# Expert rows weighted at the copy and added by indirect DMA into token sums in memory

## What is computed

```
g_idx = argmax(g_logits)                      # one of 4 groups per token
top_v, top_i = top_k(softmax(e_sel), 2)       # two of its 4 experts
combine = p_gsel * one_hot(g_idx) * e_w       # weight of each of the two
for grp in range(4):
    hid = silu(t @ w_gate[grp]) * (t @ w_up[grp])
    out = out + (hid * combine[..., None]) @ w_down[grp]
x = x + out
return rmsnorm(x, final_norm_g)
```

## Time and profile before

| | |
|---|---|
| median of 3 runs | 701.88 us (701.83 to 702.55) |
| the profiled execution | 701.97 us |
| its span on the core | 699.9 us |
| granted TensorE clock, mean | 0.993 of full speed |
| PE busy | 97% of the span |
| DVE, ACT, POOL busy | 40%, 21%, 11% |
| DMA traffic | 111.9 MB, 160 GB/s over the span |
| chain that ended last | PE 90%, DMA 4%, DVE 2% |

### The profile page before, as it was taken

One profiled execution on the slowest core, in us unless ns is written; L12 is line 12 of the kernel. 1 busy time (PEld: TensorE's weight loads), 2 busy tenths in 40 slices (PEclk: granted clock), 3 DMA queues, 4 the chain that ended last, 5 costly groups with the idle time before them and its releaser, 6 DMA issues.

```text
span 699.9 us, 8436 instructions
## 1 busy us (share of the span) xinstructions
PE 678.7 (97%) x3398; PEld 332.1 (47%) x3398; DVE 282.1 (40%) x669; ACT 144.3 (21%) x308; POOL 78.9 (11%) x106
## 2 busy tenths in 40 slices
PE   7999999999999999999999999999999999999993
PEld 4644445453557665444444555555564333333331
DVE  3107599935244665313120312323335821212156
ACT  3011251003053454211011122221111110101113
POOL 3000082312020000000000000000001110110063
PEclk9999999999999999999999999999999999999997
DMA  8803140301136513300009410630169999999673
GB/s 296 309 0 121 62 178 1 121 1 62 61 120 186 181 61 121 120 1 0 1 1 377 178 45 1 240 121 35 55 210 329 312 365 388 370 381 387 238 233 127
DMA packets 69939, 111.90 MB, mean 160 GB/s; under 512 B 5648, under 2 KB 43780, under 8 KB 69900
## 3 DMA queue, kind: packets, MB, share of 16 engines
q1 hardware_dynamic: 65724, 96.16, 39.7%
q0 software_dynamic: 4176, 15.21, 5.9%
HBM read 101.90 MB, written 9.46 MB: 159 GB/s over the span
## 4 chain that ended last, share of the span: by engine, by line
PE 90%; DMA 4%; DVE 2%; ACT 1%; POOL 1%; issue 1%; SPq 0%; DVEq 0%; POOLq 0%; ACTq 0%
PE bank L1931 19%; PE bank L2200 16%; PE bank L1806 11%; PE bank L2278 8%; PE bank L1835 5%; PE bank L1941 5%; PE bank L2288 2%; PE bank L1977 2%; PE bank L2308 2%; PE bank L2166 2%; DMA W<-y_dram,A 2%; PE bank L1963 2%; PE bank L1788 1%; PE bank L2144 1%; PE bank L2153 1%; PE bank L2049 1%
## 5 line engine op out<-in xcount | busy, mean ns | idle before, releaser
L2200 PE MATMUL bank<-W,n_sb 128*128 128x512 f32 x256 | 114.3, 596 | 0.0
L1931 PE MATMUL bank<-hT,W 128*128 128x512 f32 x240 | 104.5, 593 | 0.0
L1806 PE MATMUL bank<-W,A 128*32 128x512 f32 x672 | 84.8, 594 | 1.5 <-DVE A L1175 1.5
L2200 PEld LDWEIGHTS bank<-W,n_sb 128*128 128x128 f32 x256 | 47.3, 190 | 52.4 <-issue 52.3
L1931 PEld LDWEIGHTS bank<-hT,W 128*128 128x128 f32 x240 | 45.2, 190 | 56.1 <-issue 55.8
L2278 PE MATMUL bank<-hT,W 128*128 128x512 f32 x128 | 56.1, 592 | 0.0
L1441 DVE SCALAR_TENSOR_TENSOR A<-A,pc 128x511 f32<-128x511 f32 (+29 forms) x60 | 51.6, 860 | 2.0
L698 POOL TENSOR_TENSOR rstd<-ss,mhalf 128x1 f32<-128x1 f32 x14 | 7.7, 550 | 357.8 <-DVE ss L1068 199.0
L1806 PEld LDWEIGHTS bank<-W,A 128*32 128x32 f32 x672 | 23.1, 110 | 49.6 <-issue 47.6
L2278 PEld LDWEIGHTS bank<-hT,W 128*128 128x128 f32 x128 | 24.3, 190 | 28.1 <-issue 27.5
L1835 PE MATMUL bank<-Dn,A 128*32 128x512 f32 x264 | 36.3, 595 | 0.0
(11 more groups left out here) (311 smaller groups left out, 844.1 us busy)
## 6 DMA issues: line engine op xcount, KB each, us to landing
W<-in_w_gate_dram SPq DMA_DIRECT2D x14, 1024.0 KB, 5.4
W<-in_w_up_dram SPq DMA_DIRECT2D x14, 1024.0 KB, 10.1
Dn<-in_w_down_dram SPq DMA_DIRECT2D x11, 1024.0 KB, 14.6
W<-in_w_in_dram SPq DMA_DIRECT2D x5, 2048.0 KB, 8.6
W<-in_w_xkv_dram SPq DMA_DIRECT2D x4, 2048.0 KB, 7.9
hT<-in_w_down_dram SPq DMA_DIRECT2D x5, 1024.0 KB, 12.6
y_dram<-A POOLq DMA_DIRECT2D x10, 512.0 KB, 7.3
W<-in_w_out_dram SPq DMA_DIRECT2D x2, 2048.0 KB
```

What stands on the lines that cost most here:

```text
L1806: mm = nc.tensor.matmul(PS[2 + b][r, :], xgT[:, b, c, r], gu_at[GU_HOME[e]][:, c, :], start=c == 0, stop=c == DC - 1)
L1931: mm = nc.tensor.matmul(bank[0:w, 0:n], lhs, src[:, c, 0:n], start=c == 0, stop=c == DC - 1)
L2200: mm = nc.tensor.matmul(PS[(k + (2 if base else 0)) % 4][:, :], src[:, c, t * P:(t + 1) * P], W[:, (n_load + n) % SLOTS, c, :], start=firs ...
```

## The change

The expert rows are multiplied by their weight where they are copied out of PSUM (`y_half`: a scale on ACT, a multiplication on DVE). The weights of a pass's rows, `row_w`, come from 24 small products (`weigh_rows`): the 0/1 matrices that chose the rows, times each token's weights split into three float16 parts, put together again by DVE (`row_weights`).

Instead of `y_dram` there is `sum_dram`, 512 token rows and 128 spare rows. SP stores the residual tiles into it beside the normed ones, and once more as a filling of the spare rows. POOL adds each pass but the last to it by indirect DMA with an add: rows 0 to 95, then rows 96 to 127, since one token may be in both. Rows without a token go to spare rows of their own. Each add waits for the one before, and the gather of pass p+5 is issued between the two adds of pass p. The copies of pass p wait for the adds of pass p-2. At the end SP loads the four tiles back into `x_sb` plainly; the eight gathers and eight weighted adds are gone. Only the last pass is spread by PE (`LATE = 1`), with 0/1 matrices that need no turning; pass 10's second half is copied by DVE and not by ACT. DVE's chain of small steps in `combine` that worked out slots (L1236 to L1269) goes. The overflow branch is rewritten to add in the same way, and SP's part of it is unrolled.

```diff
-LATE = 2
-ZERO_ROW = (NP - LATE) * P
+LATE = 1
+SPLIT = 2048.0
...
-        y_dram = nc.dram_tensor("y_dram", (ZERO_ROW + 1 + OVER_PARTS * OVER_ROWS, D), F32, kind="Internal").ap()
-        y_rows = y_dram[0:ZERO_ROW, :].rearrange("(e p) d -> e p d", p=P)
-        ov_rows = y_dram[ZERO_ROW + 1:, :].rearrange("(e p) d -> e p d", p=P)
+        n_dram = nc.dram_tensor("n_dram", (S + 1, D), F32, kind="Internal").ap()
+        sum_dram = nc.dram_tensor("sum_dram", (S + P, D), F32, kind="Internal").ap()
...
                 sp.dma_start(n_dram[t * P:(t + 1) * P, :], nA[:, t, :]).then_inc(n_stored, 16)
+                sp.dma_start(sum_dram[t * P:(t + 1) * P, :], x_sb[:, t, :]).then_inc(sum_in, 16)
+                if t == 0:
+                    sp.dma_start(sum_dram[S:, :], x_sb[:, t, :]).then_inc(sum_in, 16)
...
+            sp.wait_ge(sum_in, 16 * (ST + 1))
+            for k in range(2):
+                sp.wait_ge(y_added[k], 16 * (NP - LATE))
+            for t in range(ST):
+                sp.dma_start(x_sb[:, t, :], sum_dram[t * P:(t + 1) * P, :]).then_inc(fin_in[t], 16)
...
-            def store_pass(p):
+            def add_rows(p, k):
+                r = (slice(0, CAP), slice(CAP, P))[k]
+                at = (sum_at[0:CAP, p:p + 1], sum_at_q[:, p:p + 1])[k]
+                nc.gpsimd.indirect_dma_start(out=sum_dram, out_offset=bass.IndirectOffsetOnAxis(ap=at, axis=0),
+                                             in_=ysb[r, p % 2, :], in_offset=None, compute_op=ALU.add).then_inc(y_added[k], 16)
+            def add_pass(p, between=None):
                 pool.wait_ge(y_act, p + 1)
                 pool.wait_ge(y_dve, p + 1)
-                nc.gpsimd.dma_start(y_rows[p], ysb[:, p % 2]).then_inc(y_stored[p % 2], 16)
-            for p in range(NP):
+                if p:
+                    pool.wait_ge(y_added[1], 16 * p)
+                add_rows(p, 0)
+                if between is not None:
+                    gather(between)
+                pool.wait_ge(y_added[0], 16 * p + 16)
+                add_rows(p, 1)
+            def gather(p):
                 if p >= 3:
                     pool.wait_ge(xt_ps, 2 * (p - 1))
-                if p:
-                    nc.gpsimd.indirect_dma_start(out=xg[:, p % 2, :], out_offset=None, in_=n_dram,
-                                                 in_offset=bass.IndirectOffsetOnAxis(ap=token_of[:, p:p + 1], axis=0)).then_inc(xg_in[p % 2], 16)
-                if p >= 4:
-                    store_pass(p - 4)
-            for p in range(NP - 4, NP - LATE):
-                store_pass(p)
+                nc.gpsimd.indirect_dma_start(out=xg[:, p % 2, :], out_offset=None, in_=n_dram,
+                                             in_offset=bass.IndirectOffsetOnAxis(ap=token_of[:, p:p + 1], axis=0)).then_inc(xg_in[p % 2], 16)
+            for p in range(1, 5):
+                gather(p)
+            pool.wait_ge(sum_in, 16 * (ST + 1))
+            pool.wait_ge(token_done, 3)
+            for p in range(NP - LATE):
+                add_pass(p, p + 5 if p + 5 < NP else None)
...
-            def gather_rows(slots, written):
-                for t in range(ST):
-                    for k, sl in enumerate(slots):
-                        if 2 * t + k >= 3:
-                            pool.wait_ge(fin_in[(2 * t + k - 3) // 2][(2 * t + k - 3) % 2], 16)
-                        nc.gpsimd.indirect_dma_start(out=ygath[k][:, t, :], out_offset=None, in_=written,
-                                                     in_offset=bass.IndirectOffsetOnAxis(ap=sl[:, t:t + 1], axis=0)).then_inc(fin_in[t][k], 16)
...
             def y_half(p):
                 act.wait_ge(y_ps, 2 * p + 1)
+                if p == 0:
+                    act.wait_ge(row_w_done, 1)
                 if p >= 2:
-                    act.wait_ge(y_stored[p % 2], 16 * (p // 2))
-                nc.scalar.activation(ysb[:, p % 2, 0:512], PS[5][:, :], ACT.Copy).then_inc(y_act, 1)
+                    act.wait_ge(y_added[1], 16 * (p - 1))
+                nc.scalar.activation(ysb[:, p % 2, 0:512], PS[5][:, :], ACT.Copy, scale=row_w[:, p:p + 1]).then_inc(y_act, 1)
...
-            nc.vector.tensor_copy(token_of, PS[4][:, 0:NP]).then_inc(token_done, 1)
+            nc.vector.tensor_scalar(token_of, PS[4][:, 0:NP], float(S), None, ALU.add).then_inc(token_done, 1)
             dve.wait_ge(n_stored, 16 * (ST + 1))
             turned_rows(0)
+            link(nc.vector.tensor_scalar(unused, PS[4][:, 0:NP], 0.0, rowid, ALU.is_equal, ALU.mult))
+            for r, dst in ((slice(0, P), sum_at), (slice(CAP, P), sum_at_q)):
+                nc.vector.scalar_tensor_tensor(out=dst, in0=PS[4][r, 0:NP], scalar=float(S), in1=unused[r], op0=ALU.add, op1=ALU.add).then_inc(token_done, 1)
+            for t in range(ST):
+                nc.vector.tensor_scalar(late_at[:, t:t + 1], PS[4][:, NP - 1:NP], float(S - t * P), None, ALU.add).then_inc(late_done, 1)
...
+                weight16, middle16, rest16 = (parts16[:, :, v] for v in range(3))
+                link(nc.vector.tensor_copy(weight16, weight))
+                link(nc.vector.tensor_tensor(part, weight, weight16, ALU.subtract))
+                link(nc.vector.tensor_scalar(middle16, part, SPLIT, None, ALU.mult))
+                link(nc.vector.scalar_tensor_tensor(out=part, in0=part, scalar=SPLIT, in1=middle16, op0=ALU.mult, op1=ALU.subtract))
+                nc.vector.tensor_scalar(rest16, part, SPLIT, None, ALU.mult).then_inc(parts_done, 1)
+            def row_weights():
+                dve.wait_ge(row_w_ps, 1)
+                whole, middle, rest = (PS[7][:, ST * EX + v * NP:ST * EX + (v + 1) * NP] for v in range(3))
+                link(nc.vector.tensor_scalar(row_tmp, rest, 1.0 / SPLIT, None, ALU.mult))
+                link(nc.vector.tensor_tensor(row_tmp, row_tmp, middle, ALU.add))
+                nc.vector.scalar_tensor_tensor(out=row_w, in0=row_tmp, scalar=1.0 / SPLIT, in1=whole, op0=ALU.mult, op1=ALU.add).then_inc(row_w_done, 1)
...
             def late_rows():
-                dve.wait_ge(slots_done, 2)
-                for l in range(LATE):
-                    if l:
-                        dve.wait_ge(late_done, (2 * ST + 1) * l)
-                    for t in range(ST):
-                        for k, w in enumerate((w1st, w2nd)):
-                            dst = spreadT[:, l, t] if k else late_tmp[:, t]
-                            nc.vector.tensor_scalar(dst, ranks, late_at[:, l, k, t:t + 1], w[:, t:t + 1], ALU.is_equal, ALU.mult).then_inc(late_done, 1)
-                    dve.wait_ge(late_done, (2 * ST + 1) * l + 2 * ST)
-                    nc.vector.tensor_tensor(spreadT[:, l], spreadT[:, l], late_tmp, ALU.add).then_inc(late_done, 1)
-            def late_turned(l):
-                dve.wait_ge(late_ps, l + 1)
-                nc.vector.tensor_copy(spread_w[:, l], PS[7][:, :]).then_inc(late_done, 1)
...
                 dve.wait_ge(y_ps, 2 * p + 2)
                 if p >= 2:
-                    dve.wait_ge(y_stored[p % 2], 16 * (p // 2))
-                nc.vector.tensor_copy(ysb[:, p % 2, 512:1024], PS[6][:, :]).then_inc(y_dve, 1)
+                    dve.wait_ge(y_added[1], 16 * (p - 1))
+                if p == 0:
+                    dve.wait_ge(row_w_done, 1)
+                nc.vector.tensor_scalar(ysb[:, p % 2, 512:1024], PS[6][:, :], row_w[:, p:p + 1], None, ALU.mult).then_inc(y_dve, 1)
...
-            def add_row(k, t, w):
-                dve.wait_ge(fin_in[t][k], 16)
-                if k:
-                    dve.wait_ge(fin_sum, 2 * t + 1)
-                nc.vector.scalar_tensor_tensor(out=x_sb[:, t, :], in0=ygath[k][:, t, :], scalar=w[:, t:t + 1],
-                                               in1=x_sb[:, t, :], op0=ALU.mult, op1=ALU.add).then_inc(fin_sum, 1)
...
             def add_late(t):
+                dve.wait_ge(fin_in[t], 16)
                 for n in range(2):
-                    dve.wait_ge(late_ps, LATE + 2 * t + n + 1)
...
-            def turn_late(l):
-                pe.wait_ge(late_done, (2 * ST + 1) * (l + 1))
-                if l:
-                    pe.wait_ge(late_done, LATE * (2 * ST + 1) + l)
+            def weigh_rows():
+                pe.wait_ge(parts_done, 1)
+                out = PS[7][:, ST * EX:ST * EX + 3 * NP].rearrange("p (v g j) -> p v g j", v=3, g=NG)
                 for t in range(ST):
-                    mm = nc.tensor.transpose(PS[7][:, t * P:(t + 1) * P], spreadT[:, l, t], identf[:, :])
-                mm.then_inc(late_ps, 1)
+                    w16 = parts16[:, t].rearrange("p v (g j) -> p v g j", g=NG)
+                    for j in range(3):
+                        nc.tensor.matmul(out[0:CAP, :, :, j], pick[:, t, j, :], w16[:, :, :, j], start=t == 0 and j == 0,
+                                         stop=t == ST - 1, skip_group_check=True)
+                    for j in range(3):
```

(45 more changed lines are left out.)

135 lines of the change are left out of this document (50 added, 85 removed).

## The result

The changed kernel takes 725.42 us (median of 4 runs, 724.96 to 725.84), the kernel before 702.21 beside it (701.83 to 702.77): a ratio of 1.033, 95% interval 1.0312 to 1.0348. The forecast was 715, the range 699 to 748. It is slower, by 23 us where 13 were expected.

A forecast was written before the change was run, and what follows sets the result against it. PE, with full DMA engines, bound the passes; serial transfers bound the tail. Adds in series: 567.7 + 92.4 + 34.4, reload 3.2, DVE's tail 14.8, giving 712.5; plus 2.1 around the span, 715 us, range 699 to 748.

The forecast's parts named there:

- rival A: POOL's adds in series set the end, two 7.3 us landings exceeding a pass; 715 us, own range 702 to 729, chance 0.50.
- Pass 0: Start of the add chain: first add issued at 551.9, second at 560.4 behind pass 5's gather, landed at 567.7.
- Passes 1 to 6 beside the weights: Adds while weights stream: 15.4 us a pass from two 7.3 landings and 0.8 for issue, 92.4 in all, to 660.1.
- Passes 7 to 10, without the weights: Adds after the weights are in: 4.6 + 3.2 + 0.8 = 8.6 us a pass, 34.4 in all, to 694.5.
- Reload and tail: After the last add: first tile reloaded in 3.2 us, then DVE's work to the end kept at 14.8, to 712.5.
- Rival B: In POOL's adds, reading old rows costs as much again: 23.7 us a pass, PE waiting from pass 2; 752 us, chance 0.15.
- Rival C: In the expert passes weights come late, PE 6 us late at the last up load, adds keeping pace; 707 us, chance 0.14.
- Rival D: In the expert passes the add chain keeps up with PE; 700.5 us, 699 with bare last adds, chance 0.21.
- point of decision: Threshold for the chain keeping up: 13 contended add landings between 560.4 and 671.8 us, at 6.2 us each.
- PE's lateness: PE's down products wait for adds of three passes earlier, some 5 us late by pass 6, costing nothing more.
- The other parts: Work outside the add chain, such as weighing products, scaled copies and extra tile stores: taken as nothing beside the chain.
- The rule weighed in the prediction: Skill's price for a GpSimd transfer: about 2.0 us plus bytes over 436 GB/s; two adds 5.2 us, total 698 us.

The follow-up runs named there:

- Experiment 2: Changed kernel with one add of 128 rows a pass instead of two, rows 96 to 127 going to spare rows: 707.31 us, ratio 1.0076.
- experiment 5: Changed kernel with first and second adds going to two separate tensors of sums, joined after the reload: 721.76 us, ratio 1.0266.
- Experiment 1: Changed kernel with its 22 transfers writing rows instead of adding them, same order and waits, sums not computed: 704.09 us, ratio 1.0024.
- experiment 6: Changed kernel with two tensors of sums and the last two passes spread by products, joining steps ahead of late adds: 712.03 us, ratio 1.013.
- experiment 8: Changed kernel with one plain write of 128 rows a pass instead of two adds, sums not computed: 696.74 us, ratio 0.9929.
- experiment 7: Changed kernel with only the first 8 rows of each add moved, all waits kept, sums not computed: 700.7 us, ratio 0.9975.
- experiment 3: Changed kernel with the gather of pass p+5 issued behind the second add of pass p, not between the two: 724.3 us, ratio 1.0312.
- experiment 4: Changed kernel with the last two passes spread by PE instead of one, so 20 adds instead of 22: 721.87 us, ratio 1.0286.

## Why the prediction was right, and where it was not

**The side and the mechanism (rival A, the forecast): right.** The adds in series set the end; two landings exceed a pass of 12.0 us, PE is caught by the copies, and the reload follows the last landing. Experiment 2 takes the series away, and the time is 707.31 instead of 725.42; experiment 5 keeps both adds of a pass but lets them fly together, and its passes are 12.0 us apart. The copies are held up from pass 4 on, where the prediction said pass 6.

**The size: 10.5 us short**, 712.5 against a span of 723.0. By the terms of the sum:

- Pass 0: landed at 569.5, forecast 567.7. +1.8. PE stands 1.9 us further back at the first down products (548.8 against 546.90), 1.4 of them the 24 products that weigh the rows, from 547.41 on. The prediction put these at nothing beside the chain, but they stand ahead of its start. The other 0.5 is there before the experts begin: the same products of the tokens start at 519.79 against 519.27.
- Passes 1 to 6 beside the weights: 94.8 us, forecast 92.4, 16.2 a pass against 15.4, the last of them quicker since its second add has no weights beside it. +2.4. Here two errors cancelled. "I take the contended store, 7.3, for both" gave the small transfers the price of 128 rows, and left free what an add costs over a write. Experiment 1 separates them: plain writes land in 7.1 and 5.7, together 12.8, and adding puts 2.3 on top, together 15.1. The handovers are 1.04 a pass instead of 0.8.
- Passes 7 to 10, without the weights: 39.7 us, forecast 34.4. +5.3, the term that was furthest off. "4.6 + 3.2 + 0.8" came from a bare gather and a bare store; what an add costs over a write is 2.75 a pass there and was not in it. By plain writes (experiment 1) the pass would be 7.2; it is 9.9.
- Reload and tail: 19.0 us against 18.0. +1.0. The first tile comes in 3.4 (forecast 3.2), but the third is 0.99 later than DVE wants it.

**Rival B, reading costs as much again: right in direction only.** An add does cost more than a write, but a pass beside the weights is 2.3 us longer by it and not 8.3 (23.7 less 15.4), and whether the reading is the cause stays open. Over all passes it makes up the 21 us between the change and experiment 1.

**Rival C, late weights: not in the change, but right behind it.** No expert's weights are waited for in the changed kernel, since PE is late. As soon as the adds keep pace (experiments 2, 5, 6), PE waits 5.2, 5.6 and 6.2 us for the up weights; the forecast was 6, and 707 us in all, which experiment 2 met with 707.31. That the whole fits so well is in part luck: without the adds the same kernel takes 696.74 (experiment 8), not the 701 from which C counted. The place was another: C spoke of the last up load, and the wait comes two passes earlier, at pass 9. Its ground, the bytes read once more, is not shown as bytes: the profile's MB are equal. What experiment 8 shows is that the adds take the engines' time and that without them the wait is gone.

**Rival D and its point of decision: right.** The bound was 13 contended landings of 6.2 us each. In experiment 7 the 13 take 6.2 on average and the time is 700.7 (D's number was 700.5); in experiment 1 6.5 and 704.1; in the change 7.4 and 725.4. What spoke against D in the text, the gather between the two adds, is nothing (experiment 3).

**PE's lateness** was put at 5 us by pass 6 and without effect. Its waits for copies are 11.0 us, the longest 5.2. That it costs nothing more is shown by no run; experiment 4 shows that where one pass less hangs on the chain, this second path decides.

**The other parts** were put at nothing. With the landings made short (experiment 7) the kernel is 0.25% faster than before, and with one write a pass (experiment 8) 0.7%, so they are no loss, and the gain of the tail is real. The exception is the 24 products, 1.4 us ahead of the chain. DVE's scaled copy takes 0.75 instead of 0.69.

**The rule weighed in the prediction.** Bare plain writes land in 2.51 us (32 rows) and 3.6 (96 and 128 rows), adds in 3.1 (8 rows), 3.45, 5.4 and 6.3 (128 rows); beside the weights everything is some 3 to 4 us longer. By the Trainium skill, page "DMA: Bandwidth & Descriptors", section "Anatomy of one DMA — SWDGE (gpsimd) path", the estimate for 32, 96 and 128 rows is 2.3, 2.9 and 3.2. The bare writes are within 0.7 us of that; the adds of 96 and 128 rows are about double, and beside the weights it does not hold.

## What to carry to other kernels

When a change puts transfers in series, compare the landings at the load of that stretch with the time of a pass, and then ask whether the backlog can be made good before the end: here passes of 13.4, 13.9 and 16.2 us against 12.0 left the last pass 0.2, 4.4 and 22.5 us late. Price a transfer that adds by more than its bytes: alone on the engines it held them for 3.4 us where the write took 1.3, which appears first as its own landing and, once that is hidden, as late weights elsewhere. Where each sum has few known terms, give each term a place of its own and add them on load; here that computes the same output at 0.9983 of the time before, where adding in memory takes 1.033.

## What the runs showed of the hardware that was not expected

- A landing beside full DMA engines has a large part that does not depend on its size (experiments 7 and 2 and the change): adds of 8, 32, 96 and 128 rows land in 6.1, 7.0, 8.1 and 9.5 us, where without the weights they land in 3.1, 3.45, 5.4 and 6.3. So 480 KB more (3.4 us) cost about as much as the company of the weights (3.0).
- An add costs the DMA engines time that the profile's bytes don't show: 3.4 us against 1.3 for 0.52 MB alone on them (experiments 2 and 8), and 32.0% against 21.3% for 8.39 MB beside the weights, gathers included.
- POOL is occupied for 1.3 to 1.5 us by each indirect add of the change and for 0.85 to 0.93 by the same transfer as a plain write (experiment 1).
- Between a landing and the next transfer 0.27 us pass when it is a pass's second one and 0.77 to 0.82 when it is the next pass's first (the change and experiment 1). Why was not tried.
